# Delta rule of a streaming encoder: other places for the filler passes of a head

## The reference, cut to what matters

```python
u, w = sol[..., :dv], sol[..., dv:]              # of a triangular solve by blocks
def step(s, xs):
    v_n = u_n - einsum(w_n, s)
    o = einsum(qg_n, s) + einsum(intra_n, v_n)
    s = s * gl_n + einsum(kdec_n, v_n)
ob = rmsnorm(ob, b_out_norm) * silu(zb)
gate = sigmoid(proj[..., OFF_GATE:])             # its products are the fillers
```

## Time and profile before

| | us |
|---|---|
| median of 3 runs (3427.92 to 3431.11) | 3428.77 |
| the profiled execution | 3437.7 |
| its span | 3435.9 |
| delta phase, from the first row product of head 1 to the last output sum | 1452.9 to 1991.5 |

### The profile page before, as it was taken

How to read it: one execution, slowest core, us unless ns; L and a number is a source line. 1 busy time by engine, 2 the same in 40 slices (tenths; PEclk the granted TensorE clock), 3 DMA queues, 4 the chain that set the end, 5 groups by cost and what they waited for, 6 DMA issues and landing times. The chain is left out here.

```text
span 3435.9 us, 50179 instructions
## 1 busy us (share of the span) xinstructions
PE 3254.4 (95%) x19977; PEld 3087.9 (90%) x19977; DVE 1311.4 (38%) x2289; ACT 678.8 (20%) x1318; POOL 954.7 (28%) x436
## 2 busy tenths in 40 slices
PE   6999999999999999999998979999799999999998
PEld 4999999999979888888897979978698999999997
DVE  3233232333446655554342454322225233233324
ACT  5100000000133333433323332133311000000001
POOL 3433333333322222112012033221123433333331
PEclk9999999999999999999999999999899999999999
DMA  5311111111143133111111144133401111111111
GB/s 189 137 37 42 45 42 43 43 43 37 53 148 126 55 125 138 70 60 41 64 56 71 40 164 153 31 107 137 149 31 44 44 48 41 39 42 43 37 49 56
DMA packets 95690, 250.67 MB, mean 73 GB/s; under 512 B 11456, under 2 KB 52544, under 8 KB 92864
## 3 DMA queue, kind: packets, MB, share of 16 engines
q1 hardware_dynamic: 45568, 146.95, 13.0%
q10 hardware_dynamic: 49984, 101.71, 8.2%
HBM read 198.06 MB, written 50.56 MB: 72 GB/s over the span
## 5 line engine op out<-in xcount | busy, mean ns | idle before, releaser
L129 POOL TENSOR_TENSOR w_hi<-w_raw,zero 128x1024 fp32r<-128x1024 f32 x199 | 381.3, 1916 | 2131.8 <-PE psum L162 1306.3
L162 PE MATMUL psum<-x_hi,w_hi 128*128 128x384 f32 x2952 | 584.1, 338 | 46.1 <-DVE x_lo L2314 32.0
L162 PE MATMUL psum<-x_lo,w_hi 128*128 128x384 f32 x2952 | 581.0, 336 | 0.0
L162 PE MATMUL psum<-x_hi,w_lo 128*128 128x384 f32 x2952 | 576.1, 335 | 0.0
L162 PEld LDWEIGHTS psum<-x_hi,w_hi 128*128 128x128 f32 x2952 | 520.5, 189 | 56.1 <-issue 46.1
L162 PEld LDWEIGHTS psum<-x_lo,w_hi 128*128 128x128 f32 x2952 | 521.7, 189 | 1.9
L162 PEld LDWEIGHTS psum<-x_hi,w_lo 128*128 128x128 f32 x2952 | 518.8, 188 | 0.0
L132 POOL TENSOR_TENSOR w_lo<-w_raw,w_hi 128x1024 fp32r<-128x1024 f32 x199 | 493.4, 2479 | 15.7
L414 DVE TENSOR_TENSOR f_hid<-psum,f_gate 128x384 f32<-128x384 f32 x132 | 73.6, 557 | 859.7 <-PE psum L162 857.3
L364 ACT ACTIVATE f_gate<-psum 128x384 f32<-128x384 f32 x132 | 64.8, 493 | 1479.8 <-PE psum L162 1476.1
L162 PE MATMUL psum<-f_h_hi,w_hi 128*128 128x384 f32 x1056 | 269.5, 336 | 0.0
(11 more groups left out here) (285 smaller groups left out, 3345.2 us busy)
## 6 DMA issues: line engine op xcount, KB each, us to landing
w_raw<-units SPq DMA_DIRECT2D x224, 512.0 KB, 3.5
gate_dram<-b_stash ACTq DMA_DIRECT2D x48, 192.0 KB, 1.9
e_gate<-gate_dram ACTq DMA_DIRECT2D x48, 192.0 KB, 2.5
a_kc<-k_cache ACTq DMA_DIRECT2D x4, 2048.0 KB, 7.7
a_vc<-v_cache ACTq DMA_DIRECT2D x4, 2048.0 KB, 12.9
x_sk<-mem_k ACTq DMA_DIRECT2D x8, 1024.0 KB, 8.5
proj_dram<-a_cv ACTq DMA_DIRECT2D x12, 576.0 KB, 2.7
b_pad<-proj_dram SPq DMA_DIRECT2D x12, 576.0 KB, 4.8
```

The costliest lines, as they stand in the source:

```text
L129: pool.tensor_tensor(k.w_hi[s][:, :], k.w_raw[s][:, :], k.zero[:, 0:1].to_broadcast([P, D]), ALU.add)\
L162: mm = pe.matmul(out, wl if part == 2 else wh, (xl if part == 1 else xh)[:, n0:n1], start=(part == 0 and i == 0), stop=(part == 2 and i == ...
```

## The change

Head 2 to 4: START 30 to 16, BEFORE 14 to 16, both SAMPLE places 6 to 13, END 44 to 28, and a new place of 14 behind the last output sum, on ACT evacuated behind the last root. Head 1: GROUP 18 to 20, AFTER 6 to 8, STEP 7 to 6, SAMPLE 5 to 8, END 18 to 8, LAST 8 to 6, the new place 8. No pass is added or taken away in all. Since START is shorter, each job of heads 2 to 4 ends 12 to 14 passes later in the order up to the sample: the 72nd pass is the 12th of the third group (was the 20th of the second), the 144th the last of level round 11 (was round 7), the 288th the first of the second SAMPLE place (was the second of the first one), the 360th the last of the new place. Silu of z moves to t == 4, ahead of the first key square.

```diff
-PLAN, FIRST_PLAN = (30, 22, 14, 10, (1, 2), 8, 10, 1, 6, 9), (0, 18, 14, 6, (0, 1), 8, 7, 0, 5, 8)
+PLAN, FIRST_PLAN = (16, 22, 16, 10, (1, 2), 8, 10, 1, 13, 9, 14), (0, 20, 14, 8, (0, 1), 8, 6, 0, 8, 6, 8)
...
-    def head_plan(own, units, start, group, before, after, level, w, step, behind, sample, last):
+    def head_plan(own, units, start, group, before, after, level, w, step, behind, sample, last, tail):
 
         p = own + [start] + [group] * 3 + [before, after] + list(level) * LV + [w] * 3 + [step, behind] * 8 + \
-            [sample] * 2 + [0] + [last] * 2
-        p[-3] = 3 * units * Filler.PIECES - sum(p)
+            [sample] * 2 + [0] + [last] * 2 + [tail]
+        p[-4] = 3 * units * Filler.PIECES - sum(p)
...
-                if g < 2:
-                    fill(pe, i, LAST + g)
+                fill(pe, i, LAST + g)
...
             for t in range(9):
-                if not final:
-                    if 1 <= t <= 3:
-                        silu_row(t - 1, i, 16 * i + 32)
-                    if t >= KEYS_FROM:
-                        key_square(t - KEYS_FROM, rounds + (t - KEYS_FROM), 4 * i + 7)
-                if t == 3:
+                if t == 4:
                     if isinstance(i, int) and i == 0:
                         act.wait_ge(k.z_landed.sem, k.z_landed.at(16))
                     else:
                         act.wait_ge(k.evacuated.sem, k.evacuated.at(15 * i + (6 + ND)))
                     act.activation(z[:, :], z[:, :], ACT.Silu).then_inc(k.silued.sem, 1)
                     act.preload_act_table_set("natural_log_exp_and_others")
+                if not final:
+                    if 1 <= t <= 3:
+                        silu_row(t - 1, i, 16 * i + 32)
+                    if t >= KEYS_FROM:
+                        key_square(t - KEYS_FROM, rounds + (t - KEYS_FROM), 4 * i + 7)
...
                 if g >= 2:
                     evacuate(i, LAST + g - 2)
+            evacuate(i, LAST + 2)
             act.wait_ge(k.s_final.sem, k.s_final.at(i + 1))
```

## The result

| | runs | median us | lowest to highest |
|---|---|---|---|
| before | 5 | 3428.77 | 3425.69 to 3431.40 |
| after | 5 | 3444.98 | 3443.16 to 3448.84 |

The ratio after to before is 1.0044, interval 1.0033 to 1.0055: slower, 16.2 us by the medians. The forecast was 3439 with a range of 3421 to 3450.

A forecast was written before the change was run, and what follows sets the result against it. PE, busy for 95% of the span, was taken to bound the kernel. Waits of +12.5 us, clock -4.0 and +5.4, landing -3.5 gave +10.4, added to the median 3428.77: 3439 us, range 3421 to 3450.

The forecast's parts named there:

- sample: Last key sum: 13 passes for 6 hide PE's wait in heads 1 to 3, head 4 pays 0.7; -2.2 us.
- behind the last sum: START's wait shrinks, but second groups of heads 3 and 4 give the 1.3 back; 0.3 left in head 2: -0.3 us.
- landing of head 4: Head 4's second group: its wait for the state's store and the half clock may go; -3.5 us, between 0 and -6.
- behind head 4: From PE's last work to the store of yb, 2.1 us instead of 3.4, moving the merge 1:1; -1.3 us.
- silu: Fifth step: Silu and table load ahead of the first key square make PE wait; +2.7 us, between +1 and +4.
- split behind pass 72, with head 1's: POOL's split holds DVE's masks and Y, 2.1 us in each of heads 2 to 4; head 1's other split +2.1; sum +8.4.
- split behind pass 144, evacuation behind the store: Level round 12: split delays L2010 and ACT's store, job 5's evacuation follows; +6.4 us, bounds +1 and +9.
- clock at the sample: Sample of heads 1 to 3: TensorE's half clock after idle time partly goes; -4.0 us, between 0 and -8.
- clock in new waits: Round 14's wait drops the clock (3 x 1.2), three waits of 0.7 in a row may (2 in all); +5.4 us.
- absorbed: Rival: stalls are there but absorbed, half the two splits' 14.8 us, clock falls only in round 14; 3429 us, chance 0.27.
- Opposite: Rival: POOL holds nobody that PE waits for, masks keep the port and splits run behind; 3418.5 us, chance 0.13.
- Worse: Rival: every new wait drops the clock and none of the old falls goes; 3446 to 3453 us, chance 0.10.

The follow-up runs named there:

- split_late: Kernel after, with POOL's splits behind passes 72 and 144 held in heads 2 to 4 until the head's last level is done; 3421.26 us, ratio 0.9970.
- store_late: Kernel after, with ACT storing the head before in level round 15 instead of 12; 3430.28 us, ratio 0.9996.
- late_144: Kernel after, with only POOL's split behind pass 144 held until the last level round in heads 2 to 4; 3426.19 us, ratio 0.9987.
- both_late: Kernel after, with splits behind passes 72 and 144 held behind the levels and ACT's store in round 15 instead of 12; 3413.35 us, ratio 0.9947.

## Why the prediction was right, step by step

The forecast's form held: every wait that it named is in the trace at its place, with its releaser. Its terms against the bracketed waits of the two traces, and against the busy time of the stages (a stage's busy time is held against that of a profile which has the stage at full clock; where that one has other passes, 0.173 us are counted for each):

| term | forecast | measured | 
|---|---|---|
| sample | -2.2 | -2.5 |
| END | -1.2 | -1.2 |
| behind the last sum | -0.3 | -1.5 |
| landing of head 4 | -3.5 | -0.6 of waiting, -1.3 of busy time |
| behind head 4 | -1.3 | -1.0 |
| silu | +2.7 | +3.1, alone +2.9 |
| split behind pass 72, with head 1's | +8.4 | +6.4 |
| split behind pass 144, evacuation behind the store | +6.4 | +6.8 |
| clock at the sample | -4.0 | -5.2 in heads 1 to 3 |
| clock in new waits | +5.4 | +7.3 from L1722 to L1748 of heads 2 to 4, +1.5 at the sample of head 4 |
| sum in the delta stretch | +10.4 | +11.0 |

The waits of the table sum to +9.5; the stretch has +8.5, since one wait of head 1's third group (0.45) and waits of 0.27, which no term names, are gone and the rest is rounding. With +2.5 of busy time (the table's clock and 0.2 of rests) that is 11.0.

*Mis-sized, and in each other's favour: several terms.* The direction of each is borne out, and the mechanism of each but the landing (below), but that the sum came within a microsecond of the stretch is partly luck. The new waits cost 3.4 us more clock than forecast, the split behind pass 72 cost 2.0 less, the landing gave 1.6 less and the last sum 1.2 more, and the sample 1.2 more. Where the clock falls is moreover drawn anew in part: the two profiles of the kernel before differ by 0.8 us at one sample. The recorded +5.4 is itself made of 3 x 1.2 and 2, which is 5.6.

*The term that the prediction left out.* It let head 4 pay 0.7 of new wait at the sample and no clock. The wait came (0.57), and behind it in the profile of the kernel after 1.5 us of half clock; of the seven kernels with this wait two show such a fall (this one and split_late).

*Which waits cost clock.* The prediction let three waits of 0.7 in a row cost 2 us in all. The three at L1722 (0.45 to 1.11 us each) were followed by half clock in three of twelve heads: head 3 of the kernel after and of store_late, head 4 of late_144, 1.5 to 1.6 us each, at a granted clock of 0.70 from L1722 to the first level round. In the thirty heads without these waits that stretch has 1.00. In the levels waits of 3.5 to 4.1 us were followed by a fall each time, the 1.91 us of head 2 in the kernel before too, waits of 1.06 to 1.44 never, and in head 1 a pair of 0.81 and 0.99 once (store_late) and else not. But the length of the wait alone does not tell: START's 1.60 to 1.70 us, with full passes ahead of them, cost no clock in any of nineteen places, while behind L1788, whose products have 16 columns, a wait of 0.48 us was followed by half clock in four of fourteen. What decides between these is left open by the runs.

*The split behind pass 72.* It cost 1.66 to 1.74 us of waiting a head, not 2.1, and the clock in some heads besides. The first mask lost 0.7 and the first Y 2.1 us, as drawn; PE's first wait was larger than forecast (0.69 to 0.78 for 0.6), the two behind it smaller (0.45 and 0.51 for 0.7 each), since DVE then has a third's Y ready every 1.06 us, half of which PE works.

*The split behind pass 144.* The price came out (3.78 and 3.47 us for 0.36 + 0.69 and 0.36 + 0.61), and so did head 2's (+0.9 for +0.5). That the evacuation is the smaller part and the store behind L2010 the larger was right: both_late takes all of it away.

*The last sum.* START's waits fell by 3.1 us as said, and the second groups of heads 2 and 3 took back 1.6 of them. "The gain is given back" was too strong, and the landing of head 4 was a weak term: 2.92 against 2.35 us, and 3.20, 1.52, 1.27, 3.13 and 2.44 us in other profiles. The store of the state landed in 4.3 us for 6.5, but in 4.8 with the sample alone, which has no tail: no run shows that the tail gave this back.

*Behind head 4.* 17.46 became 16.43, and 16.42 to 16.45 in each kernel with a tail.

*The median.* 16.2 us between the medians, 11.0 in the stretch. The kernel before had medians of 3430.9, 3433.4, 3431.5 and 3433.5 in the later comparisons, so its first, 3428.77 of five runs, was probably a low draw; a profile against a profile is 11.1. The forecast was added to that median, and so came out 6 us under the measured one, though the change in the stretch was the forecast one to 0.6 us.

The rivals: "absorbed" falls by the traces, since PE waited for Y in each later head and the late wait came in full in heads 3 and 4. "Opposite" falls by split_late. "Worse" had the clock of the new waits at +9.4, near the 8.8 of the kernel after, but not every new wait dropped it, and the old falls at the sample went in the main.

## What to carry to other kernels

When a plan of fillers is shifted, list what each job's end triggers on every engine (a split, an evacuation, a store) and look at whom it meets there; here that cost 24 us and hid a gain (the stretch 559.4, 534.9 with the splits held, 548.4 before; the times give 24 us and a gain of 10). A trigger with slack should not run at the earliest moment: a wait ahead of POOL's split and a later place for the store turned the slower kernel into one 0.5% faster than before. Price a wait on TensorE by the busy time behind it as well as by its length, in the stage that the edit touches and not over the whole: in one comparison here half of the 8.0 us stood where the edit had changed nothing.

## What the runs showed of the hardware

- POOL's w_lo of 128x1024 takes 2.34 to 2.40 us alone and 2.54 to 2.59 beside DVE's instructions with two inputs in SBUF; w_hi 1.89 alone, 2.13 to 2.30 beside them, and 2.87 at the sample of the kernel before. The DVE instruction that meets them goes from 0.55 or 0.60 to between 1.2 and 2.7. In the levels and at Y the loss is nearly all DVE's.
- After PE had stood still for 3.78 us the granted clock was at its 1.2 GHz level for the next products (six of L1669 in 1.49 us for 0.83), after 1.43 us in the same place it was not. At the sample a wait of 1.74 us was followed by L1797 at 3.4 to 3.8 us in heads 2 and 3 of every profile of a kernel with six passes there. With 13 passes and waits of 0.5 L1797 took 1.98 in all twenty, but in four of them the half clock had come ahead of it, 1.4 us each.
- Head 4's second group ran at half clock (1.62 us for six of L1699) each time that it had waited 2.9 to 3.2 us, four profiles. After waits of 2.3 to 2.8 us at second groups the granted clock of the next 8 us was 0.79 in three places and 1.00 in two.
- The same stretch of the same kernel took 548.39 and 548.24 us in two executions whose whole times lay 5.65 us apart. This is one pair, and in it two differences of 0.8 to 1.0 us within the stretch cancel.
